# Transposes of the FFN's hidden activations: four together, or one behind each of four steps

## The reference

```python
def swiglu_ffn(x, w_in, w_out):
    gate, up = jnp.split(x @ w_in, 2, axis=-1)
    return (jax.nn.silu(gate) * up) @ w_out

for l in range(DEPTH):
    x = x + 0.5 * swiglu_ffn(rmsnorm(x, norm_ffn1[l]), w_ffn1_in[l], w_ffn1_out[l])
    ...
    x = x + merged @ w_out[l]
    x = x + 0.5 * swiglu_ffn(rmsnorm(x, norm_ffn2[l]), w_ffn2_in[l], w_ffn2_out[l])
return rmsnorm(x, norm_final)
```

## Time and profile before

| | |
|---|---|
| median of 3 runs | 1225.2 us (1223.81 to 1225.21) |
| the profiled execution | 1225.4 us |
| its span, first to last instruction | 1223.6 us |
| granted TensorE clock, mean | 0.988 |
| TensorE busy | 1176.9 us, 5360 matmuls |
| VectorE, ScalarE, GpSimd busy | 755.6, 533.9, 56.6 us |
| read from HBM | 218.10 MB, 179 GB/s over the span |

### The profile page before, as it was taken

The page is one execution under the profiler, slowest core; times in us unless marked ns, Lnnn a source line. Parts: engine busy times, 40 slices in busy tenths (PEclk is TensorE's granted clock), DMA queues, the critical chain, the costliest instruction groups (busy, mean ns, idle before and its releaser), DMA issues.

```text
span 1223.6 us, 13278 instructions
## 1 busy us (share of the span) xinstructions
PE 1176.9 (96%) x5360; PEld 969.5 (79%) x5360; DVE 755.6 (62%) x903; ACT 533.9 (44%) x586; POOL 56.6 (5%) x73
## 2 busy tenths in 40 slices
PE   6999999999988999999999999999999699999997
PEld 5888887888866878888878888878887587888886
DVE  5554465796798664554465545467959977645442
ACT  7444345443434454443364444354433255444331
POOL 3000001000000010000020000020000001000000
PEclk9999999999988999999999999999999899999999
DMA  8655364553643455445554545545346344644440
GB/s 331 241 202 189 123 243 167 207 180 111 225 155 137 143 202 184 165 167 206 206 209 170 207 149 211 192 170 206 121 143 253 121 157 153 224 175 170 171 172 35
DMA packets 33661, 220.02 MB, mean 180 GB/s; under 512 B 3760, under 2 KB 4144, under 8 KB 8640
## 3 DMA queue, kind: packets, MB, share of 16 engines
q1 hardware_dynamic: 31104, 212.09, 47.4%
q0 software_dynamic: 1648, 6.06, 1.4%
q10 hardware_dynamic: 848, 1.02, 0.2%
HBM read 218.10 MB, written 1.05 MB: 179 GB/s over the span
## 4 chain that ended last, share of the span: by engine, by line
PE 86%; DVE 10%; ACT 2%; DMA 1%; issue 1%; SPq 0%; DVEq 0%; POOL 0%; POOLq 0%; ACTq 0%
PE acc L302 27%; PE acc L304 27%; PE acc L303 27%; DVE w_lo L884 4%; DVE y L1064 4%; PE tr L360 4%; DMA raw<-in_weights 1%; ACT w_hi L599 1%; DVE xT_lo L918 1%; ACT xT_hi L611 0%; DVE gates L1132 0%; DVE ua L1113 0%; DVE x L898 0%; PE tr L451 0%; PE tr L461 0%
## 5 line engine op out<-in xcount | busy, mean ns | idle before, releaser
L884 DVE TENSOR_TENSOR w_lo<-raw,w_hi 128x2048 fp32r<-128x2048 f32 (+2 forms) x207 | 451.1, 2212 | 108.4 <-ACT w_hi L599 107.8
L599 ACT CAST w_hi<-raw 128x2048 fp32r<-128x2048 f32 (+2 forms) x207 | 380.2, 1850 | 254.8 <-PE acc L304 252.9
L302 PE MATMUL acc<-w_hi,xT_hi 128*128 128x512 f32 x1184 | 475.8, 402 | 13.3 <-DVE gates L1132 6.3
L304 PE MATMUL acc<-w_hi,xT_lo 128*128 128x512 f32 x1184 | 465.6, 393 | 0.0
L303 PE MATMUL acc<-w_lo,xT_hi 128*128 128x512 f32 x1184 | 464.9, 393 | 0.0
L302 PEld LDWEIGHTS acc<-w_hi,xT_hi 128*128 128x128 f32 x1184 | 225.0, 190 | 59.6 <-DVE gates L1132 7.1
L304 PEld LDWEIGHTS acc<-w_hi,xT_lo 128*128 128x128 f32 x1184 | 224.4, 190 | 48.8
L303 PEld LDWEIGHTS acc<-w_lo,xT_hi 128*128 128x128 f32 x1184 | 224.9, 190 | 43.6
L937 DVE SCALAR_TENSOR_TENSOR h<-acc,rs,silu_gate 128x256 f32<-128x256 f32 x88 | 42.5, 483 | 223.0 <-ACT silu_gate L643 223.0
L302 PE MATMUL acc<-w_hi,hT_hi 128*128 128x512 f32 x352 | 137.9, 392 | 0.0
L304 PE MATMUL acc<-w_hi,hT_lo 128*128 128x512 f32 x352 | 137.1, 389 | 0.0
(11 more groups left out here) (104 smaller groups left out, 556.1 us busy)
## 6 DMA issues: line engine op xcount, KB each, us to landing
raw<-in_weights SPq DMA_DIRECT2D x195, 1024.0 KB, 4.8
raw<-in_weights SPq DMA_DIRECT2D x8, 512.0 KB, 3.4
bias<-in_gate_bias POOLq DMA_DIRECT2D x6, 512.0 KB, 7.7
raw<-in_weights SPq DMA_DIRECT2D x8, 256.0 KB, 3.6
scale_row<-in_pool_scale POOLq DMA_DIRECT2D x2, 512.0 KB, 9.1
out<-x SPq DMA_DIRECT2D x4, 256.0 KB, 2.1
x<-in_x ACTq DMA_DIRECT2D x3, 256.0 KB, 7.6
band<-in_band POOLq DMA_DIRECT2D x1, 768.0 KB, 8.8
```

What stands on the lines that cost most here:

```text
L302: nc.tensor.matmul(o, a_hi, b_hi, start=first, stop=False)
L304: return nc.tensor.matmul(o, a_lo, b_hi, start=False, stop=last)
L599: nc.scalar.copy(w_hi[:, hf % HIGHS, 0:n], raw[:, hf % RAWS, 0:n]).then_inc(hi_split, 1)
L884: nc.vector.tensor_tensor(w_lo[:, hf % RAWS, 0:n], raw[:, hf % RAWS, 0:n], w_hi[:, hf % HIGHS, 0:n].bitcast(F32), ALU.subtract).then_inc(l ...
```

## The change

`turn_h` gets a fourth argument i and makes one transpose, the i-th of the same four in the same order; the waits are made ahead of the first (i = 0), and the counter rises behind the last (i = 3). It is called from `mid` behind steps 0 to 3 of the next chunk's tile 1, in place of ahead of that tile; for the last chunk behind steps 0 to 3 (n = 0) of the first output chunk's tile 1. The functions of the other engines stay as they are.

```diff
@@ -374,11 +374,18 @@
                 pe.wait_ge(merged_all, l * 4 + 2 * t + c + 1)
                 transpose4(("m", l, t, c), [merged[:, t, c, i * P:(i + 1) * P] for i in range(4)])
 
-            def turn_h(l, f, b):
-                for t in range(T):
-                    wait_acc_taken(pe, l, f * FFN2 + b, t)
-                transpose4(("h", l, f, b),
-                           [h[:, t, c * P:(c + 1) * P] for c in (0, 1) for t in range(T)])
+            def turn_h(l, f, b, i):
+
+                name = ("h", l, f, b)
+                c, t = divmod(i, T)
+                if i == 0:
+                    for tt in range(T):
+                        wait_acc_taken(pe, l, f * FFN2 + b, tt)
+                    wait_tr_free(name)
+                mm = nc.tensor.transpose(bank(name)[:, i * P:(i + 1) * P],
+                                         h[:, t, c * P:(c + 1) * P], ident[:])
+                if i == 3:
+                    mm.then_inc(tr_full, 1)
 
             def turn_u(l, t):
                 pe.wait_ge(u_ready, l * T + t + 1)
@@ -413,8 +420,8 @@
                 in_block(l, g0, 1, norm)
                 for b in range(1, FB):
                     in_block(l, g0 + b, 0)
-                    turn_h(l, f, b - 1)
-                    in_block(l, g0 + b, 1)
+                    in_block(l, g0 + b, 1, mid={i: lambda b=b, i=i: turn_h(l, f, b - 1, i)
+                                                for i in range(4)})
                 final = len(OUT_CHUNKS) - 1
                 for i, ks in enumerate(OUT_CHUNKS):
                     g = g0 + FB + i
@@ -431,7 +438,7 @@
                                (0, 3): lambda: turn_x(*after, 0, 1)}
                     wide(l, g, g0 + FB, 0, hT, ks, i == 0, i == final)
                     if i == 0:
-                        turn_h(l, f, FB - 1)
+                        mid = {(0, j): lambda j=j: turn_h(l, f, FB - 1, j) for j in range(4)}
                     wide(l, g, g0 + FB, 1, hT, ks, i == 0, i == final, mid)
 
             def side(k, t):
```

## The result

| | before | after |
|---|---|---|
| median | 1224.7 us (1223.63 to 1226.51, 14 runs) | 1227.1 us (1225.38 to 1227.94, 14 runs) |
| ratio to before | | 1.0018, 95% interval 1.0010 to 1.0026 |
| the profiled execution, its span | 1225.4, 1223.6 us | 1226.76, 1224.9 us |

The change makes the kernel slower by 0.18%, 2.2 us by the ratio, 1.2 to 3.2 by its interval; the two medians lie 2.4 us apart. 3.2 were forecast.

What follows compares the result with a forecast made beforehand. TensorE, busy throughout the FFNs, was taken as the bound. Moving the transposes adds 0.072 us per chunk, times 44 is 3.2 us, all else 0: 1228.4 us from a median of 1225.2, range 1225.0 to 1231.5.

Steps and rivals of the forecast that it cites:

- B: FFN chunks: no change, surcharge paid once per chunk or growing with the group; 1225.2 to 1226.5 us, chance 0.26.
- D: FFN chunks: every insertion pays the whole 0.047 us surcharge; 6.2 us more, 1231.4 us, chance 0.10.
- A: FFN chunks, the forecast itself: every added insertion pays about 0.024 us; 1227.0 to 1230.0 us, chance 0.53.
- Point 3, the sum: TensorE, per FFN chunk: 0.559 us for the transposes against 0.487, 0.072 more; times 44, 3.2 us more.
- The second value that I weighed: FFN group's fourth transpose: 0.12 us by the fourth product behind it, a surcharge of 0.01 on the 0.11.
- The distance of the transposes: TensorE's FFN timeline: first transpose to next 0.815 us apart if right; 0.79 or below would show the forecast wrong.
- Rival C: FFN chunks: products hide the next transpose's load, one costs 0.057 us; 7.2 us less, 1218.0 us, chance 0.08.
- Points 4 to 7: FFN waits, later copies on ScalarE and VectorE, each FFN's last chunk, the weights' stream: cost 0 each.
- point 5: ScalarE and VectorE get transposes 2.8 us later; 0.4 us slack before the silu, 2 us on VectorE; cost 0.
- The stated reserve behind that slack: If ScalarE's slack were gone, h's late second half still has some 4 us until TensorE asks; price 0.
- Point 6: Each FFN's last chunk: ScalarE's output-stage copy moves 2.8 us, ending at 150.8, ahead of the cast at 151.60; cost 0.
- Rival E: Mixers: a later start could exchange clock cases, up to 1.4 us each; chance 0.03 of hiding or doubling the effect.

Runs made afterwards that it cites:

- eight singles: Against the changed kernel, every transpose made twice, one behind each of steps 0 to 7: period 11.893 us, 1.0186 of before's time.
- eight together: Against the changed kernel, every transpose made twice, all eight of a chunk behind step 3: period 11.788 us, 1.0155 of before's time.
- the first experiment: Against the changed kernel, the four transposes kept together behind step 3 of the next chunk's tile 1: period 11.362 us, 0.9999 of before's time.
- two chunks together: Against the kernel before, two chunks' transposes made together, eight in every second chunk: 22.67 us for two chunks, 0.9991 of before's time (0.9983 to 1.0000).

## Why the prediction was right, and where it was off

*Direction, range and mechanism held.* 1227.1 lies within 1225.0 to 1231.5. That range took in B and D too, so it tells little, and 1227.1 lies at A's low edge and below the 1227.6 from which the prediction counted a kernel as slower. It takes the 14 runs of each kernel, and the period, to tell the difference from none. Rival A's mechanism is what the traces show: each of the three added insertions per chunk pays a surcharge through the products behind it.

*Point 3, the sum, was sized too high.* I took 0.024 us for each of three insertions; over the group's own distance they pay 0.016 on the mean. Three times 44 of it make 2.2 us in place of 3.2. The size was right for the first insertion of a chunk (0.023) and too high for the second and third (0.014 and 0.012), for which no row gave a price. The second value that I weighed, 0.01 from the transposes' own tail, was a rounding: I put the fourth transpose at 67.58, the trace has 67.573 and 68.383 for the fourth product behind it, so it costs 0.130, 0.022 above the 0.108. Read to the nanosecond, both values said 0.02 to 0.025. Neither showed a second or third single. The period was forecast to grow by 0.07 us, from 11.38 to 11.45, and grew by 0.05, from 11.36 to 11.41.

*The distance of the transposes* was forecast as 0.815 us for A and 0.79 for B. It is 0.811, 0.802, 0.800, on the mean 0.804, about halfway between the two. B's form, in which the surcharge is paid once per chunk, is refuted by the prices with none, one, three and six products between, and by eight singles against eight together; its other form, a surcharge that grows with the group, by four against eight together. D (0.84) is refuted by the same distances.

*Rival C* (faster, because the load is what a transpose costs and a product would hide it) fails twice. Half the load left the distance in a group as it was, and a lone fp32r matmul, worth 0.057 us by its columns, still costs 0.12. The page "TensorE: Matmul & The Clock Gate" of the Trainium skill gives 107 ns for a load of 128 columns (section "LDWEIGHTS (loading the stationary operand)") and 56 for streaming as many (section "Back-to-back issue gap"). The fp32r matmul behind a product agrees with the first: the loads behind it stand 108 ns apart. Its own columns agree with the second: the product behind it starts 57 to 60 ns later. The transposes stream at about 0.107 per 128 columns (half the load, same distance), not at 56 ns: that figure does not hold for a float32 transpose here. With the columns at 0.108 and the next product's load at as much, there was nothing to gain by hiding a load.

*Points 4 to 7, costed at nothing*, were right, and the first experiment shows it: the same move of h's arrival without the split gives before's period. The forecasts of point 5 hold to a tenth: 0.4 us of slack ahead of the silu (0.42), 2 us ahead of VectorE's half of h (2.09). The copy was to come 2.8 us later and comes 2.77. The stated reserve behind that slack held too. With six products between, ScalarE's slack is gone, its silu 1.6 us late, and TensorE has no wait for it. Point 6 reads likewise: the copy in the output stage now ends 0.85 us ahead of the cast, which still waits for TensorE, in this profile of the changed kernel:

```profile
151.79 0.59 ACT L639 CAST hT_hi<-tr 128x512 fp32r<-128x512 f32 x1 [6.31 <-PE tr L385]
153.23 1.91 ACT L606 CAST w_hi<-raw 128x2048 fp32r<-128x2048 f32 x1 [0.85 <-PE acc L304]
```

*Rival E* names what did happen in the profiled execution, where the mixers did not keep their length: they gave back 2.0 us of the FFNs' 2.2, and the start added 1.1. The ratio of the 14 runs is the FFNs' 2.2; how long the mixers of those runs took is not on record.

**What stays open:** why products are slowed behind an insertion at all, and what sets their number, which alternates between 9 and 5 or 9 and 2 from one group of float32 transposes to the next, and why there are none behind every second small fp32r matmul; why the first of four singles costs 0.131 and the third 0.120; whether a lone transpose pays its own columns or the next product's load, both 0.108; and whether the 0.1% of two chunks together would stand in more runs.

## What to carry to other kernels

A transpose put alone between long matmuls is not hidden by them. Both short matmuls measured here with all 128 rows, the transpose and the fp32r one, fit a price of their own columns or the next operand's load, whichever is longer. Each return to the products costs something more, so few large insertions beat many small ones, here by 0.016 us for each with three products between. Before splitting a group, compare its cost per instruction with the distance inside it; only the difference can be won, and here it went the wrong way. For effects of a few tenths of a per cent, read the period of a repeated stage in the trace and not the span, in which the start and the clock move by as much as the effect.

## What the hardware showed that I had not expected

- A transpose that uses 64 of the 128 rows, alone between products that use all of them, costs 0.41 us; a whole one costs 0.124. Its load starts 0.32 us behind the product's start and not with it, and the next product's load another 0.20 us later.
- A plain float32 matmul is recorded as two matmuls with two loads, a float32 transpose of the same block as one, and the transpose's load is the shorter: 0.139 us against 0.188 to 0.192.
- Behind float32 insertions 9, 5 or 2 products run at up to 0.236 us in place of 0.227, behind every second small fp32r matmul none; the numbers alternate from one insertion to the next.
- After its idle time in the mixer TensorE's first product at 2.4 GHz came 5.60 us after it had started again in one execution and 3.95 us after in another, so a kernel that starts a stage later can end it less late.
